# The last two expert blocks finished in slot order: the tail of a mixture-of-experts trunk on one Trainium2 core

## What is computed

```python
def hier_moe(h, router_group, router_expert, w_gate, w_up, w_down):
    p_group = softmax(t @ router_group);  g_idx = argmax(p_group);  g_w = max(p_group)
    in_group = (t @ router_expert) of group g_idx
    top_w, top_i = lax.top_k(softmax(in_group), 2);  top_w = top_w / sum(top_w)
    expert_id = g_idx * EXPERTS_PER_GROUP + top_i
    combine = sum(one_hot(expert_id) * (g_w * top_w))
    for each of the 16 experts, with its column c of combine:
        hid = silu(t @ wg) * (t @ wu)
        acc = acc + c * (hid @ wd)
...
x = x + hier_moe(h, ...)
return rmsnorm(x, final_norm_w)
```

## Time and profile before

| | us |
|---|---|
| median of 3 runs | 469.94 (468.15 to 471.4) |
| the profiled execution, by its own time | 470.68 |
| its span, first to last instruction | 468.9 |
| TensorE busy in the span | 449.9 |
| VectorE, ScalarE, POOL busy | 343.5, 275.8, 158.6 |

### The profile page before, as it was taken

How to read it: one execution, slowest core, us unless ns; L and a number is a source line. 1 busy time by engine, 2 the same in 40 slices (tenths; PEclk the granted TensorE clock), 3 DMA queues, 4 the chain that set the end, 5 groups by cost and what they waited for, 6 DMA issues and landing times.

```text
span 468.9 us, 7215 instructions
## 1 busy us (share of the span) xinstructions
PE 449.9 (96%) x2797; PEld 390.8 (83%) x2797; DVE 343.5 (73%) x527; ACT 275.8 (59%) x462; POOL 158.6 (34%) x120
## 2 busy tenths in 40 slices
PE   7999999999999899999999998999999999999885
PEld 6688887899998798999999988888888888888663
DVE  4466999756767889899774357677887788778844
ACT  6753555236463162338253435689998999899443
POOL 4660000000013001114200404288878887875200
PEclk9999999999999999999999988999999999999979
DMA  8851124140202133042389512979999999998264
GB/s 306 340 225 44 78 90 140 62 159 3 89 0 92 28 119 138 32 170 100 109 349 330 209 47 56 355 295 381 376 371 353 380 371 381 356 321 323 89 219 180
DMA packets 21200, 94.57 MB, mean 202 GB/s; under 512 B 4860, under 2 KB 7080, under 8 KB 12840
## 3 DMA queue, kind: packets, MB, share of 16 engines
q1 hardware_dynamic: 14424, 83.53, 47.5%
q0 software_dynamic: 4096, 8.41, 5.4%
q10 hardware_dynamic: 2640, 2.11, 1.4%
HBM read 88.79 MB, written 11.54 MB: 214 GB/s over the span
## 4 chain that ended last, share of the span: by engine, by line
PE 69%; DVE 19%; ACT 5%; issue 3%; DMA 2%; DVEq 0%; SPq 0%; POOLq 0%; ACTq 0%
PE bank L1695 34%; PE bank L2031 6%; PE bank L2033 6%; PE bank L2032 6%; PE bank L2019 3%; DVE arena L1186 3%; DVE wl L1107 2%; PE bank L1685 2%; PE bank L1896 2%; DMA arena<-in_x_first_dram 1%; ACT wh L765 1%; PE bank L2121 1%; DMA X<-h_dram,arena 1%; PE bank L2124 1%; PE bank L1771 1%
## 5 line engine op out<-in xcount | busy, mean ns | idle before, releaser
L1695 PE MATMUL bank<-wh,acth 128*128 128x256 f32 x320 | 91.8, 287 | 0.8 <-DVE actl L1101 0.8
L1695 PE MATMUL bank<-wh,actl 128*128 128x256 f32 x320 | 90.5, 283 | 0.0
L1695 PE MATMUL bank<-wl,acth 128*128 128x256 f32 x320 | 90.5, 283 | 0.0
L1695 PEld LDWEIGHTS bank<-wh,acth 128*128 128x128 f32 x320 | 61.2, 191 | 1.1 <-issue 1.0
L1695 PEld LDWEIGHTS bank<-wl,acth 128*128 128x128 f32 x320 | 61.3, 191 | 0.0
L1695 PEld LDWEIGHTS bank<-wh,actl 128*128 128x128 f32 x320 | 61.2, 191 | 0.0
L630 POOL TENSOR_TENSOR wl<-raw,wh 128x2048 fp32r<-128x2048 f32 x4 | 20.2, 5039 | 121.3 <-ACT wh L765 121.3
L709 POOL TENSOR_TENSOR wl<-raw,wh 128x1024 fp32r<-128x1024 f32 x15 | 36.0, 2421 | 42.6 <-ACT wh L960 42.6
L2031 PE MATMUL bank<-wh,acth 128*128 128x512 f32 x124 | 50.0, 403 | 0.1
L2033 PE MATMUL bank<-wh,actl 128*128 128x512 f32 x124 | 48.7, 392 | 0.0
L2032 PE MATMUL bank<-wl,acth 128*128 128x512 f32 x124 | 48.3, 390 | 0.0
(11 more groups left out here) (378 smaller groups left out, 1044.3 us busy)
## 6 DMA issues: line engine op xcount, KB each, us to landing
arena<-in_w_gate_up_dram SPq DMA_DIRECT2D x18, 1024.0 KB, 14.0
raw<-in_w_units_dram SPq DMA_DIRECT2D x17, 1024.0 KB, 4.9
arena<-in_w_down_dram SPq DMA_DIRECT2D x16, 1024.0 KB, 11.4
raw<-in_w_gate_up_dram SPq DMA_DIRECT2D x14, 1024.0 KB, 13.4
arena<-pairs_dram SPq DMA_DIRECT2D x6, 512.0 KB, 6.6
arena<-in_x_first_dram SPq DMA_DIRECT2D x3, 768.0 KB, 7.9
arena<-in_x_dram SPq DMA_DIRECT2D x4, 512.0 KB, 12.6
arena<-in_x_dram SPq DMA_DIRECT2D x1, 2048.0 KB, 11.3
```

The lines of the kernel that those rows point to most:

```text
L1695: ins = te.matmul(acc_ap, a, b, start=(j == 0), stop=(j == n - 1))
```

## The change

1. **Gates at the block.** `slot_gates` (VectorE, in `dve_round` after the two split_b halves of block 0) computes both gates of each token and splits them times the expert masks into three bf16 parts `gvp`. `find_targets` gets 24 further products, which give `gsl`, the gate of each slot. The copies into `ysb` are scaled by it, so `pairs_dram` holds weighted rows and nothing is weighted in the tail.
2. **Order at the first block.** `find_targets` moves from ahead of the first `turn_tokens` to between `turn_tokens(1)` and `gate_up_b`, and filler before it becomes one `keep_warm(18)`. On VectorE each split_c half moves behind the following `rest_tokens`. `row_lists` makes `rix`, per tile the rows of those tokens that have no expert among blocks 14 and 15 (for the others an index out of bounds, so that the DMA leaves them out).
3. **Last two blocks.** Blocks 14 and 15 are not scattered. POOL gathers for their slots the rows of `xres` from a new copy `xres_dram` (`own_residuals`) and adds, by an accumulating gather, the first halves of the pairs (`own_first_rows`). VectorE adds `ysb`, the sum is normed in slot order, and POOL scatters it to `out`.
4. **Other tokens.** From block 13's scatter on, POOL gathers the second halves of the pairs tile by tile (`second`). Tiles 0 and 1 are added by VectorE, tiles 2 and 3 by TensorE as three identity products for each half (`xres`, first, second rows). POOL scatters each finished tile to `out`. The order of the six results is slots 14, tile 0, slots 15, tile 1, tile 2, tile 3.
5. **Loads.** `x` is copied into the second half of `pairs_dram`, and `xres` to `xres_dram` in two pieces. `load_a(3)` waits for the stores of `h2_dram` and no longer for the first gather. The load of the final norm's weights goes behind that of the first rows. The wait of `load_b` on `early_ok` goes.
6. **Ends.** `later_rounds` runs after everything else on each engine, on SP behind the wait for all six stores. The Sqrt table load moves to block 14. Some semaphores are merged.

```diff
             sp.wait_ge(hg_ev, TT)
+            sp.dma_start(pairs_dram[T:2 * T, :], x[0]).then_inc(xr_st, 16)
             sp.dma_start(xres, x[0].rearrange("(t p) n -> p t n", p=P)).then_inc(xres_in, 16)
...
-            sp.wait_ge(gat_in[0], 16)
+            sp.wait_ge(ev_dve, evacuated(n_in_groups + halves_out.index((n_front - 2, 1)))[1])
+            keep_rows(slice(0, units[n_front - 1][1]))
+            sp.wait_ge(h2_st, 16 * (n_front - n_in + 1))
             load_a(3)
+            keep_rows(slice(units[n_front - 1][1], D))
             sp_round(0, 0, True)
+            for j in range(YB):
+                sp.wait_ge(sca_out[j], (NE - G) // YB * 16)
+            wait_a(sp, 0, NE - 2)
+            sp.wait_ge(wlb_ok, (NE - 2) * 2)
+            load_first_rows()
             sp.wait_ge(h2_ok, 2 * (n_front - n_in))
             sp.dma_start(bc[:, :], final_norm_w[None, :].broadcast_to([P, D])).then_inc(ffw_in, 16)
...
+            sp.wait_ge(rows_out, OUTS * 16)
+            later_rounds(sp, sp_round, None, all_rows)
...
+            def own_residuals():
+                pool.wait_ge(xr_st, 48)
+                wait_a(pool, 0, LAST - 1)
+                pool.sem_inc(pool_tick, 1)
+                for i in range(2):
+                    gp.indirect_dma_start(own_rows[i][0:CAP, :], None, xres_dram, slots_of(LAST + i),
+                                          bounds_check=T - 1, oob_is_err=False).then_inc(own_in, 16)
+
+            def own_first_rows():
+                for j in range(YB):
+                    pool.wait_ge(sca_out[j], (NE - G) // YB * 16)
+                pool.wait_ge(own_in, 32)
+                pool.sem_inc(pool_tick, 1)
+                for i in range(2):
+                    gp.indirect_dma_start(own_rows[i][0:CAP, :], None, pairs_dram[0:T, :], slots_of(LAST + i),
+                                          bounds_check=T - 1, oob_is_err=False, compute_op=ALU.add)\
+                        .then_inc(own_in, 16)
+
+            def second(tt):
+                gp.indirect_dma_start(late[tt], None, pairs_dram,
+                                      bass.IndirectOffsetOnAxis(ap=rix[:, TT + tt:TT + tt + 1], axis=0),
+                                      bounds_check=2 * T - 1, oob_is_err=False).then_inc(gat_in[tt], 16)
+
+            def store_finished(n):
+                kind, i = finished[n]
+                pool.wait_ge(fin_ok, n + 1)
+                pool.sem_inc(pool_tick, 1)
...
                     if e + HGB < NE:
                         gather(base, e + HGB, first_round)
+                    if first_round and e >= LAST:
+                        continue
+                    if first_round and e == LAST - 1:
+                        own_residuals()
                     scatter(r, base, e)
+                    if first_round and e == LAST - 1:
+                        own_first_rows()
...
-            later_rounds(pool, pool_round)
+            for j in range(YB):
+                pool.wait_ge(sca_out[j], LAST // YB * 16)
+            pool.sem_inc(pool_tick, 1)
+            for tt in range(TT):
+                second(tt)
+            for n in range(OUTS):
+                store_finished(n)
+            later_rounds(pool, pool_round, last_scatters)
...
+                if first_round and e == NE - 2:
+                    sc.activation(dec[:, 0, 0:1], ident[:, 0:1], ACT.Sqrt)
...
-                sc.activation(ysb[e % YB][:, 0:512], bank[5][:, :], ACT.Copy).then_inc(y0_ok, 1)
+                weight = gsl[:, PERM[e]:PERM[e] + 1]
+                sc.activation(ysb[e % YB][:, 0:512], bank[5][:, :], ACT.Copy, scale=weight).then_inc(y0_ok, 1)
...
+            def slot_gates():
+                dve.wait_ge(ge_ok, 1)
+                ch.link(ve.tensor_reduce(r1[:, 6], r4[:, 1], AX_X, ALU.add))
+                dve.wait_ge(e2_ok, 1)
+                ch.link(ve.scalar_tensor_tensor(r1[:, 7], r1[:, 4], 1.0, r1[:, 6], ALU.add, ALU.mult))
+                ch.link(ve.reciprocal(r1[:, 8], r1[:, 7]))
+                ch.link(ve.tensor_tensor(r1[:, 9], r1[:, 8], r1[:, 4], ALU.mult))
+                gv = r16[:, 4:6]
+                ch.link(ve.tensor_tensor(gv, r16[:, 1:3], r1[:, 8:10].unsqueeze(3).broadcast_to([P, 2, TT, NE]),
+                                         ALU.mult))
+                for i in range(2):
+                    ch.link(ve.tensor_copy(gvp[:, i], gv))
+                    ch.link(ve.tensor_tensor(gv, gv, gvp[:, i], ALU.subtract))
+                ve.tensor_copy(gvp[:, 2], gv).then_inc(gt_v, 1)
+
+            def row_lists():
+                ch.link(ve.tensor_tensor(r1[:, 13], mb[:, :, PERM[LAST]], mb[:, :, PERM[LAST + 1]], ALU.add))
+                ch.link(ve.tensor_scalar(r1[:, 14], r1[:, 13], float(4 * T), float(NO_SLOT), ALU.mult, ALU.add))
...
                 split_b(base, 0, 0)
                 split_b(base, 0, 1)
+                if first_round:
+                    slot_gates()
+                rest_tokens(base, 0)
                 split_c(base, 0, 0)
-                rest_tokens(base, 0)
+                rest_tokens(base + 1, 1)
                 split_c(base, 0, 1)
-                rest_tokens(base + 1, 1)
...
                 if first_round:
-                    targets(0)
+                    row_lists()
+                targets(r)
                 hidden(base, 0)
...
+            for tt in range(2):
+                dve.wait_ge(row_in[tt], 32)
+                add_first(tt)
+            final_add(0)
+            for n in ADDED[1:]:
+                final_add(n)
+                final_norm(n - 1, final_rows(n - 1), n - 1)
+            final_norm(ADDED[-1], final_rows(ADDED[-1]), ADDED[-1])
+            for n in range(len(ADDED), OUTS):
+                final_norm_halves(n, finished[n][1])
+            later_rounds(dve, dve_round, None, finish_again)
...
-                keep_warm(9)
-                find_targets(r)
-                keep_warm(12)
-                turn_tokens(r, base, 0)
+                keep_warm(18)
+                turn_tokens(r, base, 0, again)
                 keep_warm(4)
                 first_gate_up_a(r, base)
-                turn_tokens(r, base, 1)
+                turn_tokens(r, base, 1, again)
+                find_targets(r)
                 gate_up_b(base, 0)
...
+            for tt, c, dst in halves_of:
+                te.matmul(dst, ident[:, :], xres[:, tt, c], start=True, stop=False)
+            for tt, c, dst in halves_of:
                 pe.wait_ge(row_in[tt], 32)
+                te.matmul(dst, ident[:, :], early[tt][:, c], start=False, stop=False)
+            for tt, c, dst in halves_of:
+                pe.wait_ge(gat_in[tt], (NE // HGB + 1) * 16)
+                te.matmul(dst, ident[:, :], late[tt][:, c], start=False, stop=True).then_inc(sum_mm, 1)
+            later_rounds(pe, pe_round, lambda: pe.wait_ge(fin_ok, OUTS))
```

266 lines of the change are left out of this document (139 added, 127 removed).

## The result

The changed kernel took 478.32 us (median of 4 runs, 477.52 to 480.65) against 469.05 us (4 runs, 468.15 to 471.4) for the kernel before: ratio 1.0192, 95% interval 1.0162 to 1.0221. It is 9.3 us slower; 471.5 us with 467 to 476 had been forecast. The profiled execution of after took 477.52 us by its own time, with a span of 475.8 us.

The account below looks back on a forecast made before the run. TensorE bounds the expert stream; the way of block 15's rows through HBM bounds the tail. Start +2.1 and tail 25.0 against 25.5 give +1.55 us of span: 471.5 us on the 469.94 median, range 467.0 to 476.0.

Parts of the forecast that it names:

- Start of the experts: First expert blocks: added VectorE work makes TensorE wait at block 1's gate_up_b, +2.1 us, bounds 1.5 and 2.6.
- Moved loads: Copies of x and xres and block 3's weights: DMA has room, first gather held 0 to 1 us, taken as 0.
- Landing of the residual gathers: Tail, POOL: both gathers land 4.0 us after their issue ends, near the empty-queue case, at 440.4.
- rival 1: Tail, slower: residual gathers land at 445.1 or later, everything from own_first_rows moves +4.7, giving 476.2; chance 0.15.
- POOL's chain behind it: Tail: block 13's scatter 436.7 to 437.7, POOL wakes 0.85 us after its releaser, second-row gathers issued from 444.65.
- The accumulating pair: Tail, POOL: two accumulating gathers at 1.4 us, 441.25 to 444.35, landing 3.4 later at 447.75; landing bounds 3.3 and 10.
- slot add 0: Tail, VectorE: first add on the own rows, starting when they land at 447.75 and ending at 449.0.
- the chain of adds and norms: Tail, VectorE: hardly waits from 447.75 on; adds of 1.25 and norms of 0.2 + 1.3 alternate, ending at 463.15.
- the end: After the last norm: POOL wakes 0.85, issues at 464.0, takes 6.05 to leave, 0.4 for closing semaphores: 470.45.
- bc at nothing: Tail, VectorE's first adds: bc load goes out at 430.2, is there by 440.4 at 10.2 us, costs 0.
- Rival 2: End, slower: SP's later_rounds jump behind the last landing stalls 4.9 us as TensorE's did, giving 476; chance 0.07.
- Rival 5: First gather: TensorE's clock falls to half again, 5 us of products take 2.5 longer, giving 474.0; chance 0.04.

Follow-up runs that it names:

- f1: Kernel before with only the change's work at the start of the experts, its tail unchanged: 471.13 us, ratio 1.0044.
- e7: Changed kernel with SP's loads of first rows and of bc held until the two residual gathers have landed: 480.58 us in one run.
- e3: Changed kernel with first rows of blocks 14 and 15 gathered plainly, without waiting for residual rows, and added by VectorE: 477.66 us in one run.
- e5: Changed kernel with accumulation removed from the two accumulating gathers, which copy instead of add: 477.8 us in one run.
- f2: Changed kernel without the four gathers of own rows (residual and first rows) and VectorE's wait for them: 468.59 us, ratio 0.9985.
- e1: Changed kernel with the load of the final norm's weights (bc) ahead of the loads of first rows: 481.64 us in one run.
- e8: Changed kernel with the bc load moved to the front, behind keep_rows: 480.61 us in one run.
- e9: Changed kernel with bc loaded in the front, plain first rows added by VectorE, and VectorE's order at the first block put back: 477.9 us, ratio 1.0196.
- e10: The three edits of e9 on the changed kernel, with the residual gathers also one block earlier: 478.0 us, ratio 1.0197.
- e2: Changed kernel with the two residual gathers one block earlier, ahead of block 12's scatter: 475.96 us in one run.
- e12: e11 plus block 13's scatter before residual gathers, plain first rows, bc before first rows, tiles 2 and 3's first rows after that scatter landed: 476.9 us, ratio 1.0145.
- e11: Changed kernel with five more filler calls ahead of the first gather, keep_warm(23) for keep_warm(18): 478.25 us, ratio 1.0175.
- f3: Changed kernel with the last two stores (tiles 2 and 3) as whole tiles from SP's queue instead of POOL's indirect ones: 477.78 us, ratio 1.0174.

## Why the prediction was wrong, step by step

- **Start of the experts, +2.1.** Right, by its mechanism and its size. Forecast 305.75 for `gate_up_b`, measured 305.64, and TensorE waits there for VectorE's split as it says; f1 gives +2.1 us (0.9 to 3.2). `row_lists` ran at the small operations' price, and the added products took 0.75 us for 24.
- **Moved loads at nothing.** Right within what was allowed: the first rows were waited for 1.51 us instead of 0.58, filled by fewer filler products; the rows themselves came at 291.32 against 291.39.
- **Landing of the residual gathers.** Here the forecast failed first. It took 4.0 us after the issue, nearer to the empty queue than to the 10.2 of the earlier trace rows, and so 440.4. Measured: 443.9, +3.5. This is the mechanism of rival 1, at three quarters of its price; e7 shows that the loads of first rows and bc cause it. The argument against rival 1, that the weights were through, counted the old traffic and not what the change adds to it: before had a DMA share of 0.84 at 430 to 435, after has 1.02. It also read the share of the earlier trace rows, 8 tenths until 434, on the clock of before, beside gather times (433.0 to 436.4) that it had itself moved back by 2.1 us: on the same clock the busy stretch ends near 436, where the issue of the two gathers does. With the loads held back (e7) the landing does take the 4.0 forecast.
- **POOL's chain behind it.** The scatter of block 13 was priced at 1.0 us and took 2.03, at no cost, as POOL waited behind it. POOL woke 0.9 us after its releaser, as forecast with 0.85. The scatter itself landed near 445, with a deadline of 449 here. In e3, where the wait ahead of the second rows is gone, they wait for it until 450.59, and still it is the first rows that VectorE waits for last.
- **The accumulating pair.** Priced as two plain DMAs of 1.4 us landing in 3.4. Measured: 2.52 + 1.51 us, landing in 5.3, so +3.1 in all with the step between them. The bounds (3.3 to 10 for the landing) held; the choice of the low one was the error. By e5 some 2.2 of these 3.1 us are the accumulation itself, which the forecast had no row for.
- The two landings and the pair's own time give slot add 0 at 454.44 for 447.75: +6.7. From there on the forecast was a little dear: 14.7 us for the chain of adds and norms from slot add 0 to the last VectorE end instead of 15.4, and 6.7 us instead of 7.3 for the end. +6.7 - 0.7 - 0.6 = +5.4 on the span, and 470.45 + 5.4 = 475.8. The rest of the 6.8 us between 471.5 and 478.32 is the choice of execution: the profiled one of before lay 0.7 above the median it was set against, that of after 0.8 below its own.
- **bc at nothing.** Wrong in the landing (14.3 us for 10.2). The 10.2 is the median of POOL's gathers, and the issues of before had a row for this very load:

```profile
bc<-in_final_norm_w_dram SPq DMA_DIRECT2D x1, 512.0 KB, 16.4
```

  Right in the cost: the 1.45 us of wait lie inside the slack of 3 us that the forecast had allowed, and in f2 bc is not waited for at all.
- **Rival 2, the jump of SP.** Wrong. After, the sequencers' branch at `later_rounds`:

```profile
L477 PEldq COMPARE_BRANCH  x1: 3790/3790/3790, 459.5 to 459.5; - x1
...
L477 SPq COMPARE_BRANCH  x1: 50/50/50, 474.5 to 474.5; - x1
```

  SP takes 50 ns for it even as the last step of all. The rule of the Trainium skill (Runtime: NRT & Kernel Launch, Instruction fetch mechanics) on taken branches shows only on TensorE here, whose 3.8 us lie hidden.
- **Rival 5, the clock.** Did not happen in after. It is real, though: e1, e3, e8, e9 and e10 show it, behind idles of 2.0 to 2.7 us, for 3.4 us each time. That costs 1.7 us and not the 2.5 priced.
- **Why no variant won.** Own rows cost 9.7 us as a chain (issue, landing, wait, issue, landing), of which each experiment took out one link; what lay beside it then became the bound: bc in e7 and e2, the landing of the first rows in e3 and e12, late weights in e2 and e10, the order at the first block in e9 and e10. What stays open is how the 8 us divide between waiting and traffic in after itself. An arrangement with residual rows placed in free memory much earlier was not tried.

## What to carry to other kernels

A DMA that is added next to the last bulk loads should be priced at the landing that busy queues show, including the traffic that the same change adds, and every link of a dependent chain of gathers pays that price again. When POOL's DMAs, a load and an engine's adds lie one behind the other within a few us, taking out one link shows little; leave the whole chain out once (f2), to see what it is worth, before mending its parts. And a step that costs TensorE 2 us in a full stream needs a tail gain of more than that to be worth anything.

## What the runs showed of the hardware beyond that

- A VectorE operation on 128 x 4 elements took 2.36 us beside a GpSimd `tensor_tensor`, 0.17 us alone (e9, after).
- Two accumulating indirect gathers of up to 112 rows of 4 KB took 2.52 and 1.51 us of POOL and landed 5.3 us later; plain ones 1.96 and 0.98 us and 4.2 us (after, e5). In e1, e7, e8 and e11 the first accumulating one took 1.56 us, and plain ones took 0.95 to 2.04.
- Two residual gathers of the same size landed 8.1 us after issue (median) beside 2.5 MB of SP's loads, 4.8 us with these held back (after, e7).
- The 512 KB load that broadcasts one row to 128 partitions took 14.3 us beside other loads (after), 17.6 in e12.
- Two whole-tile stores of 512 KB each, asked for together, landed in 4.4 us (f3).
